# A two-layer hybrid trunk on eight cores: block-diagonal recurrence gates as two full matmuls instead of four in quadrants, with a newly drawn instruction order

## The chip, the cores and the metric

The kernel runs on all 8 cores of one Trainium2 chip. Each core takes one prompt (16 learned meta tokens and 2048 prompt tokens) and 16 short sample sequences of 8 tokens: 2192 columns in all. Every core holds the same weights' program and reads them for itself. The metric is the device time in microseconds of the slowest core, the median of several executions.

## The reference, cut to what matters

Two layers, each with a feed-forward, a mixer and a second feed-forward; the change lies in the mixer's gated recurrence:

```python
for l in range(DEPTH):
    x = x + 0.5 * swiglu(rmsnorm(x, norm_ffn1[l]), w_ffn1_gu[l], w_ffn1_down[l])
    m, cb, hl, S = mixer(rmsnorm(x, norm_mix[l]), ...)
    x = x + m
    x = x + 0.5 * swiglu(rmsnorm(x, norm_ffn2[l]), w_ffn2_gu[l], w_ffn2_down[l])

def rg_lru(x, h0, pos, wa, ba, wx, bx, lam):
    xb = x.reshape(B, L, LRU_BLOCKS, LRU_BW)          # 8 blocks of 64 channels
    r = sigmoid(einsum('blnc,ncd->blnd', xb, wa).reshape(B, L, D_LRU) + ba)
    i = sigmoid(einsum('blnc,ncd->blnd', xb, wx).reshape(B, L, D_LRU) + bx)
    a = exp(-LRU_C * r * softplus(-lam))
    bt = sqrt(1 - a * a) * (i * x)                    # reset at position 0
    h_t = a_t * h_(t-1) + bt_t                        # scan over positions
```

The width is 1024, the feed-forward's 2816, the recurrence's 512: four slices of 128 channels, each of them two of the 64-wide blocks. The mixer's other half is a gated linear attention with four heads (queries and keys of 64, values of 128), in chunks.

## The kernel before, in words

Everything is kept transposed: channels on the 128 partitions, tokens along the free dimension. The residual stream `x` stays in SBUF for the whole program. The 2192 columns are cut into six tiles, `TILES`, of 256, 384, 384, 384, 400 and 384 columns, and these into two halves of three. The feed-forwards of the first half work in two tiles of 512 columns (`"w0"`, `"w1"`), the very first one from its third group of weights on; its first two groups run over tiles 0, 1 and 2 (`UNITS0`). Those of the second half work in the three tiles. In the first layer the mixer of one half is interleaved with the feed-forward of the other, and so on through the program, so that TensorE finds dense matmuls while ScalarE and VectorE work on a mixer.

Weights come from HBM, converted to bf16, over GpSimd's DMA queue into rings of slots: `rgu` (gate and up, 6 slots), `rdn` (down, 5 slots), `rpg` (the mixer's pages, 6 slots; its load is `load_page`, line 547). A slot's load is issued when the last matmul that reads the slot is done. PSUM has eight banks `ps`, given out by class (`VT`): the mixer's products are of class "M", at most four at a time.

`lru(c)` is the recurrence of one slice of 128 channels of a tile. It runs 4 slices x 6 tiles x 2 layers = 48 times. It projects, convolves on VectorE (`xc`), makes a bf16 copy `xb`, and multiplies that by the block-diagonal gate weights `bd` for `r` (first half of `bd`) and `i` (second half). Before, each of the two products is two matmuls of 64x64, one for each block, and the four of them lie in the four quadrants of the array. Block `hf` of gate `wh` lands in partitions `(hf ^ wh) * 64`, so that gate `i` comes out with its two halves of partitions exchanged. Two activations over 64 partitions each (line 991) exchange them back, while `r` is one activation of 128 partitions; its bias column is permuted to match.

No order is written by hand. `Sched` takes the list of operations, with a duration for each, and simulates the five engines: at each step it gives each engine the ready operation with the best key. The key has a priority, the length of the path behind the operation, and a perturbation: the program is cut into windows of 25,000 ns of the simulated time, and `PLAN` has a number for each, from which `policy` draws offsets for sixteen kinds of operations (`kind`), the weight of a switch of ScalarE's table, a random amount and how many banks stay for the down-projection. So the numbers in `PLAN` and the durations decide the order on every engine, the place of each DMA among GpSimd's additions, and the PSUM bank of each product. Within an engine's stream instructions run strictly in that order, with semaphore waits between engines.

Line 489 is the matmul helper, 470 the activation helper, 476 and 482 VectorE's two helpers, 592 GpSimd's addition of squares for a norm, 533 and 540 the loads of feed-forward weights, 882 the load of `bd`, once a layer.

Of the kernel before, what the change touches and what calls it, by code (L numbers as in the profile page):

```python
# [32 lines left out]
UNITS0 = [(0, 0), (0, 1), (1, 0), (1, 1), (0, 2), (1, 2)]  # L33
FIRST = ["x0", "x1", "g0", "g1", "d0", "d1", "g2", "x2", "g3", "d2", "g4", "d3", "d4", "g5", "d5", "g6", "d6", "g7", "d7", "g8", "d8"]
EARLY = 4
PLAN = [788770747, 0, 992418779, 673166238, 0, 781246477, 774010218, 0, 522389631, 334221663, 985327654, 932172178, 62324483, 0,
# [7 lines left out]
EPS = 1e-6  # L44
NCOLS = 136
NPAGE = 28
# [337 lines left out]
def build_program(cfg):  # L384
# [4 lines left out]
    wmx_d = nc.dram_tensor("wmx", [2, NPAGE, 128, 1024], F32, kind="ExternalInput").ap()  # L389
    wlr_d = nc.dram_tensor("wlr", [2, 128, 256], F32, kind="ExternalInput").ap()  # L390
    cols_d = nc.dram_tensor("cols", [128, NCOLS], F32, kind="ExternalInput").ap()
    bd_d = nc.dram_tensor("bdw", [2, 128, 512], F32, kind="ExternalInput").ap()
    wg2_d = nc.dram_tensor("wg2", [2, 128, 256], F32, kind="ExternalInput").ap()
    st0_d = nc.dram_tensor("st0", [2, 128, 256], F32, kind="ExternalInput").ap()
    S0_d = nc.dram_tensor("S0", [2, 2, 4, 128, 512], F32, kind="ExternalInput").ap()
# [8 lines left out]
    with es:  # L404
# [10 lines left out]
        cols = sb("cols_sb", [128, NCOLS], F32)  # L415
        ones = sb("ones", [128, 128], BF16)
        cst = sb("cst", [128, 928], BF16)
        bd = sb("bd", [128, 8, 64], BF16)
        wg2b = sb("wg2b", [128, 256], BF16)
        wlr = sb("wlr_sb", [128, 256], BF16)  # L420
        sm = sb("sm", [128, 64], F32)
# [42 lines left out]
        def bk(v):  # L464
            return psum[v.bank]
# [414 lines left out]
        def layer_setup(l):  # L880
            P.op("sp", lambda h: h.dma_start(out=st0[:], in_=st0_d[l]), [("go", 3, 0)], writes=["st0"], dur=60, sem=named_sem("st0"), nbytes=131072, prio=1)
            P.op("pool", lambda h: h.dma_start(out=bd[:].rearrange("p a b -> p (a b)"), in_=bd_d[l]), reads=[("go", 4, 0)], writes=["bd"], dur=600,
                 sem=named_sem("bd"), nbytes=128 * 2048, prio=1.5)
            P.op("pool", lambda h: h.dma_start(out=wlr[:], in_=wlr_d[l]), reads=[("go", 4, 0)], writes=["wlr"], dur=600, sem=named_sem("wlr"), nbytes=65536, prio=1.5)
            P.op("pool", lambda h: h.dma_start(out=wg2b[:], in_=wg2_d[l]), reads=[("go", 4, 0)], writes=["wg2b"], dur=600, sem=named_sem("wg2b"), nbytes=16384, prio=1.5)

# [5 lines left out]
        def mixer_tile(l, ti):  # L892
# [57 lines left out]
            def lru(c):  # L950
# [27 lines left out]
                else:  # L978
# [3 lines left out]
                act(xb.ap[:, :n], xc.ap[:, :n], AF.Copy, n, [xc.r], [xb.r])  # L982
                yield
                ra, it = Fa(), Fa()
                v2 = [VT("M"), VT("M")]
                P.op("pe", [mm(v2[wh], bd[hf * 64:hf * 64 + 64, wh * 4 + c, :], xb.ap[hf * 64:hf * 64 + 64, :n], n,
                               out=lambda wh=wh, r0=(hf ^ wh) * 64: bk(v2[wh])[r0:r0 + 64, :n]) for wh in range(2) for hf in range(2)],
                     [xb.r, "bd"], v2, dur=95 + 1.2 * mmd(n), prio=0)
                act(ra.ap[:, :n], lambda: bk(v2[0])[:, :n], AF.Tanh, n, [v2[0], "sm2"], [ra.r], scale=0.5, bias=sm2[:, l * 4 + c:l * 4 + c + 1], tbl="S")
                bo = 8 + l * 4 + c  # L990
                P.op("act", [lambda h, r0=r0: h.activation(out=it.ap[64 - r0:128 - r0, :n], in_=bk(v2[1])[r0:r0 + 64, :n], func=AF.Tanh, scale=0.5,  # L991
                                                           bias=sm2[r0:r0 + 64, bo:bo + 1]) for r0 in (0, 64)],
                     [v2[1], "sm2"], [it.r], dur=2 * ac(n), tbl="S", prio=1, deps=(None, None))
                xb.done()
                am = Fa()
                c1 = sm[:, l * 4 + c:l * 4 + c + 1]
# [375 lines left out]
def build_weights(inp):  # L1372
    wgu = np.empty((4, NJ, 128, 2048), np.float32)
    wdn = np.empty((4, NJ, 128, 1024), np.float32)
    wmx = np.empty((2, NPAGE, 128, 1024), np.float32)
    wlr = np.zeros((2, 128, 8, 32), np.float32)
    bdw = np.zeros((2, 128, 8, 64), np.float32)
    for l in range(2):
        for f, (gu, dn) in enumerate([(inp["w_ffn1_gu"][l], inp["w_ffn1_down"][l]), (inp["w_ffn2_gu"][l], inp["w_ffn2_down"][l])]):
            for j in range(NJ):  # L1380
                wgu[l * 2 + f, j, :, 0:1024] = _chunk_cols(gu, j * 128).reshape(128, 1024)
                wgu[l * 2 + f, j, :, 1024:2048] = _chunk_cols(gu, DFF + j * 128).reshape(128, 1024)
                wdn[l * 2 + f, j] = dn[j * 128:(j + 1) * 128, :]
        win = inp["w_in"][l]
        for k in range(12):
            wmx[l, k] = _chunk_cols(win, k * 128).reshape(128, 1024)
        for i in range(4):
            wmx[l, 12 + i] = win[i * 256:(i + 1) * 256, 1536:2048].reshape(2, 128, 512).transpose(1, 0, 2).reshape(128, 1024)
        for h4 in range(4):
            wmx[l, 16 + h4] = _chunk_cols(win, 2048 + h4 * 128).reshape(128, 1024)  # L1390
        for mc in range(8):
            wmx[l, 20 + mc] = _chunk_cols(inp["w_out"][l], mc * 128).reshape(128, 1024)
        wlr[l, :, :, :16] = _chunk_cols(win, 2560, 16)
        for wh, wname in enumerate(("lru_wa", "lru_wx")):
            for c in range(4):
                for hf in range(2):
                    bdw[l, hf * 64:(hf + 1) * 64, wh * 4 + c] = inp[wname][l, 2 * c + hf]
    return {"wgu": wgu, "wdn": wdn, "wmx": wmx, "wlr": wlr.reshape(2, 128, 256), "bdw": bdw.reshape(2, 128, 512)}

def build_cols(inp):  # L1400
    c = np.zeros((128, NCOLS), np.float32)

    def put(col, vec, nch):
        c[:, col:col + nch] = vec.reshape(nch, 128).T

    for l in range(2):
        b = l * 64
        put(b + 0, inp["norm_ffn1"][l], 8)
        put(b + 8, inp["norm_mix"][l], 8)
        put(b + 16, inp["norm_ffn2"][l], 8)  # L1410
        for k in range(4):
            put(b + 24 + k * 4, inp["lru_conv_w"][l][k], 4)
        put(b + 40, inp["lru_conv_b"][l], 4)
        put(b + 44, inp["lru_ba"][l], 4)
        put(b + 48, inp["lru_bx"][l].reshape(4, 2, 64)[:, ::-1].reshape(-1), 4)
        put(b + 52, inp["lru_lambda"][l], 4)
        put(b + 56, inp["gla_b_gate"][l], 2)
        put(b + 58, inp["gla_norm"][l], 1)
    put(128, inp["norm_final"], 8)
    return c  # L1420
# [63 lines left out]
```

How the kernel before makes its waits and increments, by code:

```python
            def body(h, name=name):  # L1347
                for k, (waits, fn, inc) in enumerate(out[name]):
                    if name == "sp" and k == past:
                        for sem, val in fin[0]:
                            h.wait_ge(sem, val)
                    for sem, val in waits[:-1] if name in ("act", "dve") else waits:
                        h.wait_ge(sem, val)
                    i = fn(h)
                    if name in ("act", "dve") and waits:
                        i = i.wait_op(waits[-1][0], waits[-1][1], "sem-ge")
                    if inc is not None:
                        i.then_inc(inc[0], inc[1])
                if name == "sp":
                    for sem, val in fin[1]:
                        h.wait_ge(sem, val)
                if name == "pool":
                    for sem in gu_sem + dn_sem + pg_sem:
                        h.wait_ge(sem, P.dcnt[id(sem)])
```

## Time and profile before

| | before |
|---|---|
| median of 3 runs | 2510.01 us (2509.41 to 2564.43) |
| profiled execution, its own time | 2509.41 us |
| its span, slowest core (core 5) | 2507.3 us |
| TensorE matmul busy | 2479.1 us, 99% |
| VectorE busy | 1533.7 us, 61% |
| ScalarE busy | 1320.1 us, 53% |
| GpSimd busy | 628.8 us, 25% |
| share of TensorE in the chain that ended last | 92% |

The profiled execution took 2.1 us more than the span of its slowest core, which is what lies around the program's own instructions. The busy time of TensorE counts a matmul from its start to its modelled end; in a dense stream each overlaps the next, so what a matmul costs is read from the distance between two starts, not from its own duration.

### The profile page before, as it was taken

To read this page: it belongs to the slowest core of one execution; us is meant where nothing else is said; L and a number is where in the kernel's file an instruction comes from. 1 tells how busy PE (TensorE), PEld (TensorE's weight loads), DVE (VectorE), ACT (ScalarE), POOL (GpSimd) and SP (SyncE) were. 2 spreads that over 40 slices of the span, in tenths; PEclk is the share of its full clock that TensorE was granted. 3 is DMA by queue.
4 is the path that set the end of the run, shared out by engine and by line. 5 is a ranking of instruction groups with operands and counts; after the bars stand their busy time and mean duration, and the time that the engine had idled before them with its cause. 6 is when DMAs were issued, how large, how long until landed. Compare 5 with 4: busy or idle time off the path is not lost.

```text
span 2507.3 us, 42427 instructions; the slowest of 8 cores (2499.4 to 2507.3 us)
## 1 busy us (share of the span) xinstructions
PE 2479.1 (99%) x14673; PEld 1349.2 (54%) x14673; DVE 1533.7 (61%) x3016; ACT 1320.1 (53%) x2507; POOL 628.8 (25%) x1011
## 2 busy tenths in 40 slices
PE   7999999999999999999999999999999999999998
PEld 4444565555544444444555556655554444555556
DVE  6444765657766679444753367666576666886346
ACT  2312678676868675311311148685678686753114
POOL 2212331213322313301200042422151413142002
PEclk9999999999999999999999999999999999999999
DMA  9666577666867897465344447767566787786322
GB/s 186 125 109 93 93 119 108 99 103 96 121 102 110 124 150 129 74 94 85 60 72 68 65 75 106 120 100 118 94 99 104 109 126 112 143 134 138 51 43 78
DMA packets 118173, 259.28 MB, mean 103 GB/s; under 512 B 12912, under 2 KB 23664, under 8 KB 117968
## 3 DMA queue, kind: packets, MB, share of 16 engines
q0 software_dynamic: 104576, 238.38, 61.2%
q1 hardware_dynamic: 12672, 17.59, 2.1%
q8 instruction: 127, 2.08, 0.3%
q14 instruction: 78, 0.64, 0.1%
q10 hardware_dynamic: 720, 0.59, 0.1%
HBM read 472.21 MB, written 13.65 MB: 194 GB/s over the span
## 4 chain that ended last, share of the span: by engine, by line
PE 92%; ACT 4%; DVE 1%; issue 1%; DMA 1%; POOL 0%; DVEq 0%; POOLq 0%; ACTq 0%
PE ps L489 91%; PE ps L488 1%; ACT Fb L470 1%; DMA rgu<-wgu 1%; DVE x L476 1%; ACT L470 1%; ACT Fb L991 1%; ACT L999 0%; ACT sg L470 0%; ACT Bb L470 0%; ACT Fb L999 0%; PE ps L1194 0%; DVE Fb L476 0%; ACT Fb L1000 0%; POOL x L498 0%
## 5 line engine op out<-in xcount | busy, mean ns | idle before, releaser
L489 PE MATMUL ps<-xn,rgu 128*128 128x384 bf16 (+4 forms) x6896 | 1312.9, 346 | 1.2 <-DMA rgu<-wgu 0.9
L489 PEld LDWEIGHTS ps<-xn,rgu 128*128 128x128 bf16 x6896 | 669.9, 98 | 574.4 <-issue 7.7
L476 DVE SCALAR_TENSOR_TENSOR x<-ps,x 128x384 f32<-128x384 f32 (+5 forms) x1056 | 609.0, 601 | 239.2 <-PE ps L489 220.3
L489 PE MATMUL ps<-hb,rdn 128*128 128x384 bf16 (+4 forms) x3384 | 677.5, 346 | 0.7 <-ACT Fb L470 0.3
L470 ACT ACTIVATE sg<-ps 128x384 f32<-128x384 f32 (+5 forms) x451 | 234.2, 525 | 787.2 <-PE ps L489 672.9
L482 DVE TENSOR_TENSOR hb<-ps,sg 128x384 bf16<-128x384 f32 (+5 forms) x451 | 266.8, 600 | 386.4 <-PE ps L489 330.9
L489 PEld LDWEIGHTS ps<-hb,rdn 128*128 128x128 bf16 x3384 | 327.0, 98 | 276.5 <-issue 8.6
L547 POOL DMA_DIRECT2D rpg<-wmx x336 | 180.1, 539 | 683.2 <-PE ps L489 621.4
L489 PE MATMUL ps<-xnt,rpg 128*128 128x384 bf16 (+3 forms) x1536 | 262.1, 318 | 0.4 <-ACT Fb L470 0.3
L533 POOL DMA_DIRECT2D rgu<-wgu x168 | 90.7, 540 | 615.3 <-PE ps L489 602.0
L470 ACT ACT_TABLE_LOAD x149 | 191.2, 1283 | 26.0 <-PE ps L489 21.6
L489 PEld LDWEIGHTS ps<-xnt,rpg 128*128 128x128 bf16 x1536 | 147.5, 98 | 94.5 <-issue 3.4
L470 ACT ACTIVATE sqf<-x 128x384 bf16<-128x384 f32 (+3 forms) x244 | 106.7, 471 | 142.6 <-DVE x L482 69.7
L540 POOL DMA_DIRECT2D rdn<-wdn x166 | 88.8, 546 | 324.9 <-PE ps L489 319.9
L476 DVE SCALAR_TENSOR_TENSOR Fb<-Fb,cols_sb 128x384 f32<-128x384 f32 (+3 forms) x216 | 122.8, 577 | 72.6 <-ACT Fb L470 39.3
L470 ACT ACTIVATE Fb<-ps 128x384 f32<-128x384 f32 (+5 forms) x262 | 112.9, 463 | 37.9 <-PE ps L489 28.5
L489 PE MATMUL ps<-mixin,rpg 128*128 128x384 bf16 (+3 forms) x768 | 126.0, 319 | 0.0
L476 DVE SCALAR_TENSOR_TENSOR Fb<-Fb 128x384 f32<-128x384 f32 (+2 forms) x144 | 84.3, 587 | 68.0 <-ACT Fb L991 42.5
L476 DVE SCALAR_TENSOR_TENSOR xn<-x,cols_sb,ps 128x256 bf16<-128x256 f32 (+3 forms) x216 | 105.7, 547 | 8.4 <-ACT ps L625 8.4
L489 PEld LDWEIGHTS ps<-mixin,rpg 128*128 128x128 bf16 x768 | 75.3, 98 | 46.3 <-issue 1.3
L592 POOL TENSOR_TENSOR rsf<-rsf,sqf 128x384 f32<-128x384 f32 (+3 forms) x116 | 91.8, 807 | 32.1 <-ACT sqf L470 31.3
L592 POOL TENSOR_TENSOR rsf<-sqf 128x384 f32<-128x384 bf16 (+3 forms) x58 | 47.6, 821 | 127.6 <-ACT sqf L470 120.0
(141 smaller groups left out, 1757.8 us busy)
## 6 DMA issues: line engine op xcount, KB each, us to landing
rgu<-wgu POOLq DMA_DIRECT2D x168, 512.0 KB, 7.3
rpg<-wmx POOLq DMA_DIRECT2D x336, 256.0 KB, 6.5
rdn<-wdn POOLq DMA_DIRECT2D x166, 256.0 KB, 7.2
x<-xT POOLq DMA_DIRECT2D x8, 768.0 KB, 9.8
yT<-Fb SPq DMA_DIRECT2D x24, 192.0 KB, 5.0
rpg<-wgu POOLq DMA_DIRECT2D x7, 512.0 KB, 9.5
S0f<-S SPq DMA_DIRECT2D x12, 256.0 KB, 8.9
Sos<-S0f SPq DMA_DIRECT2D x12, 256.0 KB, 5.1
```

The lines of the kernel that those rows point to most:

```text
L470: P.op("act", lambda h: h.activation(out=o_(), in_=i_(), func=func, scale=scale, **kw), reads, writes, dur=ac(n, ptr, 0 if callable(in_) e ...
L476: P.op("dve", lambda h: h.scalar_tensor_tensor(out=o_(), in0=a_(), scalar=scalar, in1=b_(), op0=op0, op1=op1), reads, writes, dur=dv(n, 0 ...
L482: P.op("dve", lambda h: h.tensor_tensor(out=o_(), in0=a_(), in1=b_(), op=op), reads, writes, dur=dv(n), prio=prio, port=not (callable(in0) ...
L488: return lambda h: h.matmul(o_(), lhsT=lhsT, rhs=rhs, start=start, stop=stop, skip_group_check=True)
L489: return lambda h: h.matmul(o_(), lhsT=lhsT, rhs=rhs, start=start, stop=stop)
L533: P.op("pool", lambda h: h.dma_start(out=s.ap.rearrange("p (a b) -> p a b", a=2), in_=wgu_d[fi, j].rearrange("p (a b) -> p a b", a=2)), wr ...
L540: P.op("pool", lambda h: h.dma_start(out=s.ap, in_=wdn_d[fi, j]), writes=s.keys, dur=600, sem=s.sem, nbytes=128 * 1024 * 4, prio=prio)
L547: P.op("pool", lambda h: h.dma_start(out=rpg[:, s, :], in_=wmx_d[l, k]), reads=[("go", 5, min(pg_n[0] // 3, 2))], writes=[("pg", s)], dur= ...
L592: P.op("pool", lambda h: h.tensor_tensor(out=out, in0=a, in1=b, op=ALU.add), reads, writes, dur=pl(self.n), prio=0, port=True)
L991: P.op("act", [lambda h, r0=r0: h.activation(out=it.ap[64 - r0:128 - r0, :n], in_=bk(v2[1])[r0:r0 + 64, :n], func=AF.Tanh, scale=0.5, bias ...
```

## The change

The gate product of `lru` becomes one full 128x128 matmul for each of the two gates. The weight page `bd` holds each pair of blocks as a 128x128 matrix with zeros beside the diagonal, so it has 8 x 128 columns instead of 8 x 64, and its DMA reads 512 KB instead of 256 KB of float32 from HBM. Each gate has its own bank, taken when its matmul is given out, and one activation over 128 partitions. The bias of gate `i` is not permuted any more. The duration that `Sched` is told is twice one matmul's instead of `95 + 1.2 * mmd(n)` for the four. `PLAN` has other numbers throughout, of which a line is shown. The tiling of the feed-forwards, the rings and all other operations are as before.

```diff
-PLAN = [788770747, 0, 992418779, 673166238, 0, 781246477, 774010218, 0, 522389631, 334221663, 985327654, 932172178, 62324483, 0,
+PLAN = [301746851, 0, 1013753834, 374752431, 0, 211164062, 689418677, 0, 0, 919143051, 683213839, 630184684, 126345493, 892550642,
...
-        bd = sb("bd", [128, 8, 64], BF16)
+        bd = sb("bd", [128, 8, 128], BF16)
...
-                 sem=named_sem("bd"), nbytes=128 * 2048, prio=1.5)
+                 sem=named_sem("bd"), nbytes=128 * 4096, prio=1.5)
...
-                v2 = [VT("M"), VT("M")]
-                P.op("pe", [mm(v2[wh], bd[hf * 64:hf * 64 + 64, wh * 4 + c, :], xb.ap[hf * 64:hf * 64 + 64, :n], n,
-                               out=lambda wh=wh, r0=(hf ^ wh) * 64: bk(v2[wh])[r0:r0 + 64, :n]) for wh in range(2) for hf in range(2)],
-                     [xb.r, "bd"], v2, dur=95 + 1.2 * mmd(n), prio=0)
-                act(ra.ap[:, :n], lambda: bk(v2[0])[:, :n], AF.Tanh, n, [v2[0], "sm2"], [ra.r], scale=0.5, bias=sm2[:, l * 4 + c:l * 4 + c + 1], tbl="S")
-                bo = 8 + l * 4 + c
-                P.op("act", [lambda h, r0=r0: h.activation(out=it.ap[64 - r0:128 - r0, :n], in_=bk(v2[1])[r0:r0 + 64, :n], func=AF.Tanh, scale=0.5,
-                                                           bias=sm2[r0:r0 + 64, bo:bo + 1]) for r0 in (0, 64)],
-                     [v2[1], "sm2"], [it.r], dur=2 * ac(n), tbl="S", prio=1, deps=(None, None))
+                for wh, dst in ((0, ra), (1, it)):
+                    v = VT("M")
+                    P.op("pe", mm(v, bd[:, wh * 4 + c, :], xb.ap[:, :n], n), [xb.r, "bd"], [v], dur=mmd(n), prio=0)
+                    bo = wh * 8 + l * 4 + c
+                    act(dst.ap[:, :n], lambda v=v: bk(v)[:, :n], AF.Tanh, n, [v, "sm2"], [dst.r], scale=0.5, bias=sm2[:, bo:bo + 1], tbl="S")
...
-                    bdw[l, hf * 64:(hf + 1) * 64, wh * 4 + c] = inp[wname][l, 2 * c + hf]
+                    bdw[l, hf * 64:(hf + 1) * 64, wh * 4 + c, hf * 64:(hf + 1) * 64] = inp[wname][l, 2 * c + hf]
...
-        put(b + 48, inp["lru_bx"][l].reshape(4, 2, 64)[:, ::-1].reshape(-1), 4)
+        put(b + 48, inp["lru_bx"][l], 4)
```

What the order looks like on TensorE where the recurrence of the second mixer tile's first two slices runs among a feed-forward of the other half (`xn,rgu` is its gate or up product, `xnt,rpg` and `rpg,xnt` projections of the mixer, `vtm,kendT` the attention's state update, which writes 64 partitions for each head). Before:

```order
L489 MATMUL ps<-rpg,xnt 128x512 x8
L489 MATMUL ps<-Bb,bd 64x384 x4
L489 MATMUL ps<-rpg,xnt 128x512 x16
...
L489 MATMUL ps<-xn,rgu 128x400 x8
L489 MATMUL ps<-xn,rgu 128x384 x16
L489 MATMUL ps<-Bb,bd 64x384 x4
L489 MATMUL ps<-vtm,kendT 64x128 x6
```

And in the changed kernel, at the same two gate products:

```order
L489 MATMUL ps<-rpg,xnt 128x512 x8
L489 MATMUL ps<-Bb,bd 128x384 x2
L489 MATMUL ps<-rpg,xnt 128x512 x16
...
L1190 MATMUL ps<-cst,Bb 128x128 x3
L489 MATMUL ps<-xn,rgu 128x400 x8
L489 MATMUL ps<-Bb,bd 128x384 x2
L489 MATMUL ps<-vtm,kendT 64x128 x6
```

Each gate product is two rows' worth of full matmuls at nearly the same place; what stands before the second one has changed. In the whole stream 7 of the 48 gate products stand directly before `vtm,kendT` before, and 8 of 48 now.

On VectorE at the very start of the program (squares of tile 1, `sqf<-x 128x384`, among the normalized columns of tile 0, `xn 128x256`, and of tile 1), before:

```order
L482 TENSOR_TENSOR sqf<-x 128x384
L476 SCALAR_TENSOR_TENSOR xn<-x,cols_sb,ps 128x256 x3
L482 TENSOR_TENSOR sqf<-x 128x384
L476 SCALAR_TENSOR_TENSOR xn<-x,cols_sb,ps 128x256 x2
L482 TENSOR_TENSOR sqf<-x 128x384
L476 SCALAR_TENSOR_TENSOR xn<-x,cols_sb,ps 128x384 x8
L482 TENSOR_TENSOR hb<-ps,sg 128x256 x2
```

Now:

```order
L476 SCALAR_TENSOR_TENSOR xn<-x,cols_sb,ps 128x256 x3
L482 TENSOR_TENSOR sqf<-x 128x384 x2
L476 SCALAR_TENSOR_TENSOR xn<-x,cols_sb,ps 128x256 x5
L482 TENSOR_TENSOR sqf<-x 128x384
L476 SCALAR_TENSOR_TENSOR xn<-x,cols_sb,ps 128x384 x4
L482 TENSOR_TENSOR hb<-ps,sg 128x256
L476 SCALAR_TENSOR_TENSOR xn<-x,cols_sb,ps 128x384 x4
```

The last square of tile 1 now stands behind five normalizations of tile 0 in a row, and on TensorE the matmul that takes it stands behind the first six of the first feed-forward product.

On GpSimd where `bd` is loaded for the first time and the mixer's pages begin, before:

```order
L882 DMA bd<-bdw 128x512
L885 DMA wg2b<-wg 128x256
L884 DMA wlr_sb<-wlr 128x256
L540 DMA rdn<-wdn 128x1024 x3
L498 DMA x<-xT 128x4x384 x2
L533 DMA rgu<-wgu 128x2048 x3
L547 DMA rpg<-wmx 128x1024 x2
L540 DMA rdn<-wdn 128x1024 x2
L547 DMA rpg<-wmx 128x1024 x4
```

Now:

```order
L885 DMA wg2b<-wg 128x256
L884 DMA wlr_sb<-wlr 128x256
L882 DMA bd<-bdw 128x1024
L540 DMA rdn<-wdn 128x1024 x3
L498 DMA x<-xT 128x4x384 x2
L533 DMA rgu<-wgu 128x2048 x3
L547 DMA rpg<-wmx 128x1024 x2
L540 DMA rdn<-wdn 128x1024 x2
L547 DMA rpg<-wmx 128x1024 x3
L533 DMA rgu<-wgu 128x2048
L547 DMA rpg<-wmx 128x1024
```

The larger load of `bd` goes behind two small ones, and one load of a feed-forward slot has moved ahead of the sixth page. Shifts of this size run through the whole stream: of about 500 rows on GpSimd and 1500 on TensorE most stand a few places away from where they stood.

## Rows read from the trace of the kernel before

**Rows 1.** The cores' spans and mean granted TensorE clock.

```profile
core 1: 2500.4 us, clock 0.999
core 5: 2507.3 us, clock 0.995
die 0 (median of its cores): 2500.2 us, clock 0.999
die 1 (median of its cores): 2506.9 us, clock 0.995
```

**Rows 2.** Windows of core 5, all engines (PE, PEld, DVE, ACT, POOL busy, clock, DMA).

```profile
60.00:2480.00 2420.00, 2415.43 (x14166) 1305.38 (x14165) 1480.89 (x2882) 1289.03 (x2439) 606.82 (x973) 1.00 0.63 101
```

**Rows 3.** What PE waited for from 60 to 2480 us (total, times, longest).

```profile
PE ps L489 <- ACT Fb L470: 0.7, 2, 0.3
PE ps L489 <- DVE hb L482: 0.6, 2, 0.4
PE ps L489 <- DVE Bb L476: 0.6, 1, 0.6
PE ps L489 <- POOL Bb L592: 0.6, 2, 0.3
PE ps L488 <- DVE Fb L476: 0.5, 2, 0.3
PE ps L489 <- DVE Bb L482: 0.5, 1, 0.5
```

**Rows 4.** PE in order of time, core 5: start, duration, count, idle before.

```profile
19.05 2.83 PE L489 MATMUL ps<-xn,rgu 128*128 128x256 bf16 x16
22.73 0.49 PE L489 MATMUL ps<-xn,rgu 128*128 128x256 bf16 x3 [0.85 <-DMA rgu<-wgu]
...
54.11 1.46 PE L489 MATMUL ps<-xn,rgu 128*128 128x384 bf16 x8
55.41 1.14 PE L489 MATMUL ps<-hb,rdn 128*128 128x384 bf16 x6
...
2471.17 5.40 PE L489 MATMUL ps<-xn,rpg 128*128 128x256 bf16 x48
2476.41 0.33 PE L489 MATMUL ps<-sqf,ones 128*128 128x400 bf16 x1
```

**Rows 5.** PE around a gate product of 384 columns.

```profile
430.80 0.98 PE L489 MATMUL ps<-xn,rgu 128*128 128x384 bf16 x5
431.70 0.36 PE L489 MATMUL ps<-Bb,bd 64*64 64x384 bf16 x4
431.99 0.85 PE L489 MATMUL ps<-hb,rdn 128*128 128x400 bf16 x4
432.68 0.33 PE L489 MATMUL ps<-xnt,rpg 128*128 128x384 bf16 x1
```

**Rows 6.** PE around a gate product of 256 columns.

```profile
277.61 0.81 PE L489 MATMUL ps<-xn,rgu 128*128 128x384 bf16 x4
278.35 0.30 PE L489 MATMUL ps<-Bb,bd 64*64 64x256 bf16 x4
278.58 0.82 PE L489 MATMUL ps<-rpg,xnt 128*128 128x512 bf16 x3
```

**Rows 7.** PE where a gate product stands beside a state update.

```profile
408.71 1.14 PE L489 MATMUL ps<-xn,rgu 128*128 128x384 bf16 x6
409.78 0.36 PE L489 MATMUL ps<-Bb,bd 64*64 64x384 bf16 x4
410.06 0.36 PE L489 MATMUL ps<-vtm,kendT 128*64 128x128 bf16 x6
410.36 1.15 PE L489 MATMUL ps<-xn,rgu 128*128 128x384 bf16 x6
```

**Rows 8.** ACT's groups for the gates of 384 columns (busy, mean ns, idle before).

```profile
L991 ACT ACTIVATE Fb<-ps,sm 64x384 f32<-64x384 f32 x64 | 36.9, 576 | 2.7 <-PE ps L489 1.1
L470 ACT ACTIVATE Fb<-ps,sm 128x384 f32<-128x384 f32 x32 | 18.5, 578 | 12.4 <-PE ps L489 12.3
```

**Rows 9.** DMA issues: KB each, median us to landing; and GpSimd's additions.

```profile
rpg<-wmx POOLq DMA_DIRECT2D x336, 256.0 KB, 6.5
L592 POOL TENSOR_TENSOR rsf<-rsf,sqf 128x384 f32<-128x384 f32 (+3 forms) x116 | 91.8, 807 | 32.1 <-ACT sqf L470 31.3
```

**Rows 10.** POOL's page loads in order of time, and PE's use of them.

```profile
622.26 0.54 POOL L547 DMA_DIRECT2D rpg<-wmx  x1 [5.71 <-PE ps L489]
...
627.99 1.46 PE L489 MATMUL ps<-xnt,rpg 128*128 128x384 bf16 x8
```

**Rows 11.** Windows of core 5, PE alone: busy, granted clock, DMA share, GB/s.

```profile
33.00:48.00 15.00, 14.74 (x82) 0.81 1.06 170
249.00:264.00 15.00, 15.00 (x70) 0.81 0.29 50
350.00:365.00 15.00, 15.00 (x88) 0.81 0.92 144
```

More of the change, by code:

```diff
@@ L391, in build_program @@
     cols_d = nc.dram_tensor("cols", [128, NCOLS], F32, kind="ExternalInput").ap()
-    bd_d = nc.dram_tensor("bdw", [2, 128, 512], F32, kind="ExternalInput").ap()
+    bd_d = nc.dram_tensor("bdw", [2, 128, 1024], F32, kind="ExternalInput").ap()
     wg2_d = nc.dram_tensor("wg2", [2, 128, 256], F32, kind="ExternalInput").ap()
@@ L1376, in build_weights @@
     wlr = np.zeros((2, 128, 8, 32), np.float32)
-    bdw = np.zeros((2, 128, 8, 64), np.float32)
+    bdw = np.zeros((2, 128, 8, 128), np.float32)
     for l in range(2):
@@ L1396, in build_weights @@
                 for hf in range(2):
-                    bdw[l, hf * 64:(hf + 1) * 64, wh * 4 + c] = inp[wname][l, 2 * c + hf]
-    return {"wgu": wgu, "wdn": wdn, "wmx": wmx, "wlr": wlr.reshape(2, 128, 256), "bdw": bdw.reshape(2, 128, 512)}
+                    bdw[l, hf * 64:(hf + 1) * 64, wh * 4 + c, hf * 64:(hf + 1) * 64] = inp[wname][l, 2 * c + hf]
+    return {"wgu": wgu, "wdn": wdn, "wmx": wmx, "wlr": wlr.reshape(2, 128, 256), "bdw": bdw.reshape(2, 128, 1024)}
 def build_cols(inp):
```

14 rows, old and new, of the table PLAN are left out of this document.

## The prediction

> **What bounds the kernel now.** I read the cores first, then the busy shares by stage, then what TensorE waits for, and last the distances between its matmuls. The cores say which one to look at: core 5 of the second die, 2507.3 us, while the first die needs 2500.2 us [rows 1]. That gap is no work of the program. Three stretches of 15 us on core 5 were granted a TensorE clock of 0.81, between the chip's two levels of 1.2 and 2.4 GHz, in the middle of dense matmuls [rows 11]; a matmul stream slowed to 0.81 loses 0.19 of each stretch, 3 x 15 x 0.19 = 8.5 us, about the 6.7 us by which the dies differ.
>
> The stage view leaves one engine. From 60 to 2480 us TensorE is busy for 2415.4 of 2420 us, VectorE for 1481, ScalarE for 1289, GpSimd for 607 [rows 2]. TensorE's idle time there is the 3.5 us of the waits view, six kinds with a longest of 0.6 us [rows 3]. So the time is the sum of TensorE's distances from start to start, plus some 23 us before the steady stream and 8 us after it. An engine beside TensorE can return at most the few microseconds of rows 3, and a microsecond of TensorE's stream is a microsecond of the kernel. A gain of 50 us (2%, about what a measurement of this kernel can tell from no change) isn't there to be had by an edit of 48 small products.
>
> The price of a plain matmul comes from two neighbours in time: eight of 384 columns from 54.11 to 55.41 us, 0.163 us each; forty-eight of 256 from 2471.17 to 2476.41, 0.109 us each [rows 4]. For 400 columns I take 400/384 of the first, 0.170.
>
> **The gate products on TensorE.** This is the term that carries the sum. Four 64x64 matmuls show a busy time of 0.36 us together, barely over one matmul's own 0.347, so they run side by side. What they cost is seen in their neighbours [rows 5]. From 430.80 five plain matmuls ought to last 5 x 0.163 = 0.81 us, and the quadrants begin after 0.90: 0.09 us lost ahead. The next plain matmul starts 0.29 us after them. The four of 400 behind need 0.69 instead of 0.68: 0.01. In all 0.39 us. Two full matmuls of 384 cost 2 x 0.163 = 0.326. The edit therefore returns 0.064 us for a product of 384 columns, though it doubles the columns streamed through the array: the quadrants save 0.163 us of streaming and pay about 0.23 us for entering and leaving their mode. At 256 columns [rows 6]: 0.74 - 0.65 = 0.09 ahead, 0.23 inside, 0.01 behind, 0.33 in all against 0.218, a return of 0.11. At 400 it is 0.40 against 0.340, a return of 0.06.
>
> Seven products stand directly before the attention's state update, which writes 64 partitions and has to leave the full mode anyway. There the entry is shared [rows 7]: 1.07 - 6 x 0.163 = 0.09 ahead, 0.28 for the quadrants, 0.30 for the update; the update alone would keep 0.09 + 0.30, so the product costs 0.28 there, and two full matmuls cost 0.045 us more. In the new order eight products stand there, at no extra price, since the update pays for its own entry.
>
> The sum: 48 products are 32 of 384 columns, 8 of 400 and 8 of 256; 25 x 0.064 + 8 x 0.06 + 8 x 0.11 - 7 x 0.045 = 1.60 + 0.48 + 0.88 - 0.32 = 2.6 us less on TensorE. All of it is on the path.
>
> The Trainium skill speaks against this edit: "TensorEngine Tiling (Array Packing)", section Theoretical Speedup, gives 2x for each dimension of at most 64 and hence four quadrants in the time of one. Its section Key Properties says that a change of tiling mode drains the engine, without a price. By the first alone each product would now cost a whole matmul more; the trace agrees that the four run side by side and puts a price of about 0.23 us on the drain, which is the larger of the two.
>
> **ScalarE.** Gate `i` was two activations of 64 partitions, 0.576 us each, as long as the one of 128 for `r`, 0.578 [rows 8]. One instead of two returns about 0.57 x 48 = 27 us of busy time (somewhat less at 256). It lies beside TensorE's work: 1289 of 2420 us are busy. What it can give is a shorter recurrence chain, at most the waits in rows 3 that come from the mixer's chain. I book 0 and keep the whole of rows 3 for the range.
>
> **DMA and banks.** `bd` is 256 KB more, once a layer; a page of 256 KB lands in 6.5 us [rows 9], and the first gate product comes at 278 us, over 100 us after the load's place in GpSimd's stream. Nobody waits for it; its price without that cover would be some 6 us, once. The two gates take their banks one after the other instead of both at once, which can only ease the limit of four.
>
> **The start.** VectorE now makes the last square of tile 1 after five normalizations. Each of these takes 0.43 us, so the square comes some 0.8 us later, and the matmul that takes it splits the first feed-forward product. Before, TensorE was done with the first sixteen at 21.9 and stood 0.85 us, to 22.73, for the second slot of weights [rows 4]. The loads' order up to there is unchanged, so 22.73 stands and the delay falls into that wait. Price without the cover: 0.8 us. The normalized columns of tile 1 come 1.2 us later too, near 25.5; the product that needs the last of them gets there at 22.73 + 16 x 0.109 + 7 x 0.163 = 25.6. I book 0, and up to 1 us in the range.
>
> **The new order.** It touches everything, and no row prices it beforehand. What it can change is TensorE's idle time and the small losses around it. Below: all of rows 3 gone, 3.5 us, and as much again because a matmul that starts after a wait isn't overlapped by the one before (0.163 us a time, over 20 places), so -7 us. Above: twice as much waiting, +7 us, is my bound for an order that hides as well as the old one. I take 0: both orders have the same dependencies and the same engines at 25 to 61% beside TensorE.
>
> Sum: 2509.41 - 2.6 = 2506.8 us against the profiled execution. The median of the runs is 0.6 higher, and I forecast **2507 us**.
>
> **The rivals.**
>
> *Page loads slip (slower).* The mixer's weights arrive with nothing to spare. The page issued at 622.26 lands by the median of 6.5 us at about 628.8, or a little earlier, and the product that starts at 627.99 is of its kind [rows 9, 10]; six slots and a rule of "issue when the last reader is done" make this the normal case. If the new order puts one more of GpSimd's additions (0.807 us) ahead of a page that is used on landing, TensorE stands for that long. Once in each of the 12 mixer tiles this is 12 x 0.81 = 9.7 us: 2516.5 us; twice, 2526. It decides from the point at which issue to first use drops under the landing time. Against it: the page loads wait for TensorE nearly always, not for an addition, and rows 3 show no wait for a page at all. Chance 0.15.
>
> *The mixer's chain stops showing.* ScalarE's 27 us and single banks remove the waits that come from mixer products. All of rows 3 and the restart losses gone: 2506.8 - 7 = 2500 us. For it: five of the six rows of waits name a mixer buffer or a norm. Against: other waits would take their place. Chance 0.12.
>
> *The packing rule holds.* The 0.09 us ahead and the tail behind a quadrant group belong to neighbours that would be there anyway, and a full product costs a whole matmul more: +0.163 x 32 + 0.17 x 8 + 0.109 x 8 = 7.5 us, 2517 us. Against it: the same loss ahead in rows 5, 6 and 7 with three different followers. The section Theoretical Speedup of "TensorEngine Tiling (Array Packing)" in the Trainium skill would have it so. Chance 0.05.
>
> *No gain, since the mode changes stay.* If the two full matmuls were separated by tiled work, or the drain moved to whoever is next, the time would be 2509.5 us. In the order nearly all pairs stand together, 40 of 48 between full matmuls. Chance 0.08.
>
> **How the numbers follow.** The forecast (2503 to 2511) has 0.58, the rivals 0.15, 0.12, 0.05 and 0.08, and 0.02 is for something large. The clock adds a width of its own: without the three stretches of 0.81 the slowest core would be at the first die's 2500; with twice as many it would be 8 us above. The range of 2499 to 2516 takes in the low rival, the packing rule nearly, the lower part of the first rival and most of the clock's width, and leaves out about 2 in 10. All cases but the last lie within 2%: same 0.97, slower 0.02, faster 0.01.
>
> **What the next profile would show.** The gate product as two of 128x384 with 0.326 us from its start to the next matmul's and no loss ahead: if there is a loss, the first step is wrong. TensorE's busy time 3 to 4 us lower, 14,577 matmuls; ScalarE's about 27 us lower. TensorE's waits between 60 and 2480 us near 3.5 us: over 10 us, above all for pages, would be the first rival. The first sixteen matmuls of the feed-forward ending in a wait for weights to 22.7 us. Stretches at 0.81: as many as before, or the comparison of the slowest cores is off by 2.8 us for each. Wrong altogether would be a stage in which TensorE stands for several microseconds.

## The result and the profile after

The changed kernel took 2497.3 us (median), the kernel before 2509.9 us beside it: 0.995 of it, 95% interval 0.9928 to 0.9973, so 12.6 us less. In two later comparisons on other chips it was 0.9960 (0.9944 to 0.9976) and 0.9962 (0.9950 to 0.9975), 10.1 and 9.6 us less. Every time and difference from here on is a median over the executions in which no die ran long at a lower clock, while the expectations quoted below reckon with medians over all executions, which lie up to 1 us beside them. The direction was forecast, the size was not: 2.6 us were expected, and 2497.3 lies under the range's lower end of 2499.

The changed kernel's page: the share of each engine, the chain that ended last, and the cores' spans, which answer to [rows 1].

```profile
span 2496.5 us, 42211 instructions; the slowest of 8 cores (2490.1 to 2496.5 us)
PE 2473.0 (99%) x14577; PEld 1357.6 (54%) x14577; DVE 1522.7 (61%) x3016; ACT 1287.1 (52%) x2459; POOL 628.5 (25%) x1011
PE 98%; DVE 1%; DMA 0%; ACT 0%; POOL 0%; issue 0%; DVEq 0%; ACTq 0%; POOLq 0%
die 0 (median of its cores): 2490.9 us, clock 0.999
die 1 (median of its cores): 2494.7 us, clock 0.997
```

TensorE's share of the chain went from 92 to 98%; ScalarE's, 4% before, is gone. ScalarE's busy time is 33 us lower, where 27 were forecast. The undisturbed die went from 2500.2 to 2490.9 us.

TensorE's stage from 60 to 2480 us (window), what it waited for there (waits), and a gate product in order of time; these answer to [rows 2], [rows 3] and [rows 5].

```profile
60.00:2480.00 2420.00, 2418.82 (x14182) 1322.05 (x14181) 1475.08 (x2896) 1260.86 (x2402) 608.33 (x974) 1.00 0.62 102
```

```profile
PE ps L489 <- DVE xn L476: 1.0, 5, 0.2
```

```profile
418.92 1.46 PE L489 MATMUL ps<-xn,rgu 128*128 128x384 bf16 x8
420.21 0.49 PE L489 MATMUL ps<-Bb,bd 128*128 128x384 bf16 x2
420.54 1.46 PE L489 MATMUL ps<-xnt,rpg 128*128 128x384 bf16 x8
```

Eight matmuls take 1.29 us to the gate's start, 0.161 each: nothing is lost ahead. The two full ones take 0.33. The ten waits of the kernel before are gone; eight of them ended on a mixer buffer or a norm, two on a feed-forward's hidden values `hb`. The five that are left, 0.2 us each, are of another place, the normalized columns of a feed-forward's first product at 2244 us.

**Where the time went.** Rows of idle time understate a wait: the matmul after it is not overlapped by the one before. And a matmul can start late with so little idle time, or none, that the waits view doesn't list it at all; the shortest that it lists is 0.2 us. In the kernel before, ahead of a projection of the mixer:

```profile
282.44 1.63 PE L489 MATMUL ps<-hb,rdn 128*128 128x384 bf16 x9
284.10 1.03 PE L489 MATMUL ps<-xnt,rpg 128*128 128x256 bf16 x8
```

Nine of 384 columns need 9 x 0.163 = 1.47 us and the next starts after 1.66: 0.19 us are lost, and no idle time stands beside the second row. So I added, over all matmuls, the distance from each start to the next less the distance that its shape has in a dense stream (0.163 us at 384 columns, 0.216 at 512, 0.169 at 400, 0.109 at 256), and sorted the rest by what stands there. For core 5, 2507.3 us before and 2496.3 after:

| part of core 5's difference | us |
|---|---|
| the 48 gate products, with what they cost their neighbours | -2.4 |
| TensorE kept waiting between 22 us and the end, restarts included | -4.6 |
| stretches of lower clock | -2.3 |
| from the last matmul to the last store | -1.4 |
| the first 22 us | -0.3 |
| sum | -11.0 |

How the sum is divided between clock, waits and products is good to about half a microsecond, since a matmul in a slow stretch can have waited as well. Core 1 ran at full clock on both sides and is the cleaner of the two: of its 10.0 us, 2.3 are the products with their neighbours, 5.5 the waits, 2.0 the way from the last matmul to the last store and 0.2 the first 22 us. Of the waits the larger part was never in [rows 3]: from 60 to 2470 us on core 5 the late starts that the waits view doesn't list came to 5.4 us before and 1.7 after.

The clock term is in the windows of the changed kernel, which answer to [rows 11]. The stretch at 33 us is missing and the two others are there. The rows are of core 4, the slowest; there, behind the waits at 2244 us, 3.4 us more ran at 0.50, the lower of the two levels. Core 5 of the table had no such stretch.

```profile
248.00:263.00 15.00, 15.00 (x70) 0.81 0.33 57
348.00:363.00 15.00, 15.00 (x96) 0.82 0.74 124
2247.00:2250.40 3.40, 3.40 (x13) 0.50 0.24 78
```

That leaves two causes to tell apart. The waits can have gone because the edit takes work from ScalarE, or because the new numbers drew a better order.

### The profile page after: what moved, and what is told of

Same layout as the page of the kernel before. It is cut to its first block, busy times and chain, and to the rows that moved or that the text cites. A ratio compares the mean times of both kernels' runs of the same rounds, so it can differ in the third digit from the quotient of the medians.

```text
span 2496.5 us, 42211 instructions; the slowest of 8 cores (2490.1 to 2496.5 us)
## 1 busy us (share of the span) xinstructions
PE 2473.0 (99%) x14577; PEld 1357.6 (54%) x14577; DVE 1522.7 (61%) x3016; ACT 1287.1 (52%) x2459; POOL 628.5 (25%) x1011
## 4 chain that ended last, share of the span: by engine, by line
PE 98%; DVE 1%; DMA 0%; ACT 0%; POOL 0%; issue 0%; DVEq 0%; ACTq 0%; POOLq 0%
PE ps L489 97%; PE ps L488 1%; DMA rgu<-wgu 0%; DVE xn L476 0%; PE ps L1190 0%; DVE x L476 0%; POOL x L498 0%; DVE S0f L476 0%; DVE sqf L482 0%; ACT L624 0%; ACT Bb L470 0%; ACT ps L624 0%; ACT Fb L470 0%; ACT ps L625 0%; DVE hb L482 0%
```

## The experiments

The old order can be kept exactly. It follows from the durations told to the scheduler and from `PLAN`, not from the instructions, so one operation of two full matmuls with the old duration leaves every engine's stream as it was. All the runs named "old order" have that stream, instruction by instruction, and those named "new order" the changed kernel's. Each was measured against the kernel before on the same chip.

**Run 1: the edit in the old order.** The kernel before, with

```diff
-                P.op("pe", [mm(v2[wh], bd[hf * 64:hf * 64 + 64, wh * 4 + c, :], xb.ap[hf * 64:hf * 64 + 64, :n], n,
-                               out=lambda wh=wh, r0=(hf ^ wh) * 64: bk(v2[wh])[r0:r0 + 64, :n]) for wh in range(2) for hf in range(2)],
+                P.op("pe", [mm(v2[wh], bd[:, wh * 4 + c, :], xb.ap[:, :n], n) for wh in range(2)],
...
-                P.op("act", [lambda h, r0=r0: h.activation(out=it.ap[64 - r0:128 - r0, :n], ...) for r0 in (0, 64)],
-                     [v2[1], "sm2"], [it.r], dur=2 * ac(n), ...)
+                P.op("act", [lambda h: h.activation(out=it.ap[:, :n], ...)],
+                     [v2[1], "sm2"], [it.r], dur=2 * ac(n), ...)
```

> The gate products are two full 128x128 matmuls and one activation for each gate, as in the changed kernel, but the order of every engine is that of the kernel before, instruction by instruction, since the durations told to the scheduler and PLAN are the old ones. Theory 1 (the edit returns what its 48 products cost less on TensorE, and the drawn order returned the rest): 2.4 to 2.8 us less than the kernel before on each die, near 2507, TensorE's idle time after the start still about 3.5 us, ScalarE's busy time some 27 us lower. Theory 2 (the 27 us of ScalarE's time shorten the mixer's chain, and that removed the waits): 6 to 8 us less than before, near 2503, with TensorE's idle time after the start close to the 1.3 us of the changed kernel.

Measured: 2496.1 against 2504.7 us, 0.9964 (0.9950 to 0.9978), so 8.6 us less. Theory 1 is out; theory 2 had the right side and named too little. A chip later, beside the changed kernel itself:

> The edit in the old order once more, beside the changed kernel on one chip. It gave 9.0 us in its first run, the changed kernel 9.6 us on another chip. If the drawn order adds nothing, both lie within 1 us of each other here; if it adds what the first comparison suggested, the changed kernel is 2 us or more ahead.

Measured: 2494.2 against 2503.8 us, 0.9963 (0.9950 to 0.9976), 9.6 us less. And the changed kernel on that chip and on the one before it:

> The changed kernel, unaltered, beside the run before this one: 9 to 10 us less than the kernel before, 0.996 of it, and 0 to 1 us less than the edit in the old order. Its gain on the first chip was 12.3 us, of which 2 to 3 us would be stretches of lower clock if this theory is right, so no more than 10.5 here unless the kernel before shows three such stretches again.

> The changed kernel once more, unaltered, beside the next two kernels and the kernel before on one chip, to see what the drawn order adds to the edit. The edit alone, in the old order, gave 9.0 us against the kernel before on the chip of the runs before this one. Theory 1 (the drawn order returned most): 12 us less than before, with 3 us or more from the order. Theory 3 (the edit gives nearly all in either order, and the rest of the first comparison lay in stretches of lower clock and in the last store): 9 to 11 us less than before.

Measured: 2494.2 against 2503.8, 0.9962 (0.9950 to 0.9975), and 2493.3 against 2503.4, 0.9960 (0.9944 to 0.9976). On the one chip that ran both, the drawn order adds nothing to the edit: 9.6 us with it and 9.6 without. The 12.6 us of the first comparison had some 2 to 3 us of clock in them, as the table shows for core 5; the two later profiles of the changed kernel have a mean clock of 0.999 on every core.

**Run 2: ScalarE's part put back.** As run 1, but gate `i` by two activations of 64 partitions, without the exchange.

```diff
+                P.op("act", [lambda h, r0=r0: h.activation(out=it.ap[r0:r0 + 64, :n], in_=bk(v2[1])[r0:r0 + 64, :n], ...) for r0 in (0, 64)],
```

> As the run before it, but gate i is still made by two activations of 64 partitions each, without the exchange, so that ScalarE has as much to do as in the kernel before; only TensorE's products change. Theory 1: the same time as the run before it within 0.5 us, some 2507. Theory 2: 2507 as well, but 4 to 5 us slower than the run before it. TensorE's busy time in both as in the changed kernel; 0.326 us for a product of 384 columns and nothing lost ahead of it.

Measured: 2500.4 us, 0.9982 (0.9972 to 0.9992): 4.3 us less than the kernel before, 4.3 more than run 1. That is the step of 4 to 5 us that theory 2 named; the level, 2507, is too high in both theories. The waits view of the slowest core hardly tells the two runs apart, 2.2 us in 6 waits against 2.3 in 7; the late starts that it doesn't list went from 1.7 to 4.8 us on core 5.

**Run 3: ScalarE's part alone.** The kernel before, quadrants and all, with one activation for gate `i`; the exchange of the two halves of partitions is left out.

> The kernel before, in its own order and with its four quadrant products, but gate i is made by one activation over 128 partitions. It leaves out the exchange of the two halves of partitions, so gate i goes to the wrong half of the channels; the work of every other instruction is as before. It takes ScalarE's 27 us alone out of the kernel before. Theory 3 (a shorter ScalarE leg in the recurrence removes half of TensorE's waits): 4 to 5.5 us less than before. Theory 1 (ScalarE is covered): 0 to 1 us less.

Measured: 2496.6 against 2503.4 us, 0.9973 (0.9962 to 0.9984), 6.9 us less, more than either theory named. Without any change to TensorE's products, most of the gain is there.

**Run 4: work given back to ScalarE, at another place.** Run 3 with an idle copy of 64 partitions added where the scan is over.

```diff
+                    P.op("act", [lambda h: h.activation(out=scr[:, :n], in_=hs.ap[0:64, :n], func=AF.Copy, scale=1.0),
+                                 lambda h: h.activation(out=hprev[:, c:c + 1], in_=hs.ap[:, n - 1:n], func=AF.Copy, scale=1.0)],
```

> The run with the old order, the quadrants and one activation for gate i (whose exchange of the two halves is left out), which took 6.8 us off the kernel before, with 48 idle copies of 64 partitions added on ScalarE just before the copy of the scan's last column. ScalarE is as busy as in the kernel before, but the work stands behind the recurrence's chain instead of in its middle. If ScalarE's occupancy as such makes TensorE wait, all of the 6.8 us come back and it equals the kernel before. If only the length of the leg from the gate product to the scan counts, it stays 5 to 7 us below. In between if other chains of the mixer run behind that place on ScalarE.

Measured: 2498.2 against 2503.8 us, 0.9979 (0.9969 to 0.9988), 5.6 us less. ScalarE is busy for 1303 us instead of 1286, which is only half of the way back to the 1320 of the kernel before, so the expectation's "as busy as" was not met. If occupancy as such were the price, about 3.4 of the 6.9 us would have come back; 1.2 did, across two chips. So most of the gain is not ScalarE's occupancy, but where in the recurrence the work stands. In the traces of core 1 the time from a gate product's first matmul to the end of the last exponential, mean of 48, is 7.07 us before, 6.23 in run 3, 6.26 here, 6.30 in run 1 and 5.96 in the changed kernel. One activation less is 0.8 us off that leg.

**Run 5: one activation more.** Run 2 with gate `r` in two halves as well.

> The full products in the old order, with two activations of 64 partitions for gate i and two for gate r, none of them exchanging halves: ScalarE has 27 us more to do than in the kernel before and 54 more than with one activation a gate. If each 27 us of ScalarE's work in the chain costs alike, 4 to 6 us more than with three activations (which was 4.1 us below before), so equal to the kernel before or up to 2 us above. If the waits have a floor and the first 27 us were just at an edge, 1 us or less more.

Measured: 2520.9 against 2503.4 us, 1.0071 (1.0057 to 1.0084), 17.5 us more. The leg is 7.77 us. What TensorE waited for from 60 to 2480 us:

```profile
PE ps L489 <- DVE Bb L476: 2.4, 3, 1.2
PE ps L488 <- DVE Fb L476: 2.3, 3, 0.9
PE ps L489 <- DVE hb L482: 2.2, 5, 0.7
PE ps L489 <- DVE mixin L476: 2.2, 5, 0.6
PE ps L488 <- ACT Sb L470: 1.3, 2, 0.7
```

Three of these five kinds stand in [rows 3] too; in all there are 39 waits of 20.7 us against 10 of 3.5. With two, three and four activations the edit in the old order stands at -8.6, -4.3 and +17.5 us. The price of one more half activation for each product (29 and 34 us of ScalarE's busy time) went from 4.3 to 21.8 us, and the listed waits from 7 to 39: in an order cut close, a further delay of the same length finds many more places without slack.

One place shows it. It is where the attention's first product of the tile of 400 columns waits for `Bb`, TensorE's rows in order of time, here in the kernel before:

```profile
766.19 1.03 PE L489 MATMUL ps<-hb,rdn 128*128 128x512 bf16 x4
767.85 0.45 PE L489 MATMUL ps<-Bb 64*16 64x16 bf16 x8 [0.63 <-DVE Bb L476]
```

Four of 512 columns take 4 x 0.216 = 0.86 us, so 0.80 us are lost ahead of the second row. In run 1:

```profile
758.35 1.03 PE L489 MATMUL ps<-hb,rdn 128*128 128x512 bf16 x4
759.30 0.45 PE L489 MATMUL ps<-Bb 64*16 64x16 bf16 x8
```

0.09 us are lost, and no wait: as much as ahead of the quadrants in [rows 5], the entry into the smaller mode. In run 2:

```profile
759.70 1.03 PE L489 MATMUL ps<-hb,rdn 128*128 128x512 bf16 x4
761.17 0.45 PE L489 MATMUL ps<-Bb 64*16 64x16 bf16 x8 [0.44 <-DVE Bb L476]
```

0.61 us. And in run 5:

```profile
763.65 1.03 PE L489 MATMUL ps<-hb,rdn 128*128 128x512 bf16 x4
765.90 0.45 PE L489 MATMUL ps<-Bb 64*16 64x16 bf16 x8 [1.23 <-DVE Bb L476]
```

1.39 us. So this place alone follows the leg step by step. This product isn't of the recurrence at all. How the leg's length reaches it is in the chain that ended last, of the kernel before, its longer pieces in order of time from 746 us:

```profile
746.57 0.60 ACT Fb L991
749.22 1.28 ACT L999
750.52 0.72 ACT Fb L999
751.24 0.61 ACT Fb L1000
...
758.95 1.28 ACT L1113
760.24 0.60 ACT Fb L1113
...
763.76 1.28 ACT L1130
766.14 0.97 DVE Bb L476 x3
767.87 2.56 PE ps L489 x20
```

It begins with a half activation of gate `i` (L991), goes on through the recurrence's exponentials (L999, L1000) and only then comes to the attention's (L1113, L1130), whose result VectorE needs for `Bb`: ScalarE works them off in its queue's order.

**Runs 6 and 7: the new order.** The changed kernel with the quadrants and two activations back, and with full products and two activations.

```diff
-                    P.op("pe", mm(v, bd[:, wh * 4 + c, :], xb.ap[:, :n], n), [xb.r, "bd"], [v], dur=mmd(n), prio=0)
+                    P.op("pe", [mm(v, bd[hf * 64:hf * 64 + 64, wh * 4 + c, hf * 64:hf * 64 + 64], xb.ap[hf * 64:hf * 64 + 64, :n], n,
+                                   out=lambda v=v, r0=(hf ^ wh) * 64: bk(v)[r0:r0 + 64, :n]) for hf in range(2)],
+                         [xb.r, "bd"], [v], dur=mmd(n), prio=0)
```

> The new order, instruction by instruction, with the gate products in the four quadrants of 64x64 again and two activations of 64 partitions for gate i, so that what is left of the change is the drawn order alone. Theory 1: 2.4 to 2.8 us slower than the changed kernel, near 2500, and still about 9 us faster than the kernel before; TensorE's idle time after the start near 1.5 us. Theory 2: TensorE's waits come back with ScalarE's longer work, 2504 to 2506. If a pair of products does not run side by side in the new order, because it is given out as two operations, it costs up to 0.16 us more for each such product.

> The changed kernel's order and full products, with two activations of 64 partitions for gate i. The quadrants with two activations in this order were 4.4 us slower than the kernel before, and the changed kernel 9.6 us faster, so products and activations together are worth 14 us in this order. If the activations carry most of it, as 4.9 of 9.0 us in the old order, this one lies 7 to 9 us above the changed kernel; if the products do, 3 us above it.

Measured: 2509.4 against 2504.7 us, 1.0017 (1.0008 to 1.0026), 4.7 us more than the kernel before and above what either theory named; and 2500.1 against 2503.8, 0.9985 (0.9976 to 0.9994), 3.7 us less, between the two cases. So the new order with the old work is worse than the old order, and the edit is worth 14 us in it: 5.9 for the activation and, across two chips, 8.4 for the products. Of the 8.4 about 2.4 are TensorE's own; the rest is waiting time, 5.6 us more than before in run 6 on core 1 by the sum of distances, and 0.6 less in run 7. In the old order too the products gave more than their own 1.9 us when ScalarE had three activations (4.3 us), and 1.8 to 2.7 when it had two. Why full products spare TensorE waits beyond their own time was not settled: the leg is as long with them (7.02 us in run 2, 7.07 before).

**Runs 8 and 9: other draws.** The changed kernel with the `PLAN` of the kernel before, and with `PLAN = [0]`.

> The changed kernel with the PLAN numbers of the kernel before: another drawn order for the same work. If any order hides the work beside TensorE as well as any other, within 2 us of the changed kernel, 2496 to 2500. If the new PLAN is a particularly good draw, the waits of TensorE after the start come to 5 to 20 us and the time to 2503 to 2520.

> The changed kernel with a PLAN of zeros, so that no window's order is perturbed: the order that the durations and priorities alone give. With the numbers of the kernel before the changed kernel took 60 us more than with its own, TensorE standing for several microseconds at a time around 1870 and 2240 to 2310 us. If that is what an order costs that isn't picked for its durations, this one lies 30 to 90 us above the changed kernel, with TensorE idle in the same places; if the old numbers were an unlucky draw, within 15 us.

Measured: 2565.7 us, 1.0243 (1.0223 to 1.0262), 61 us more than the kernel before, hence some 70 more than the changed kernel and far above both cases; and 2548.7 us in one execution against 2503.4, 45 us more than the kernel before and 55 more than the changed kernel. TensorE's longest kinds of waits, from 60 to 2480 us, with the old numbers:

```profile
PE ps L489 <- DVE mixin L476: 13.0, 3, 6.5
PE ps L489 <- DVE xn L476: 8.8, 5, 4.2
```

and with zeros:

```profile
PE ps L482 <- DVE xn L469: 14.2, 6, 4.6
PE ps L482 <- DVE x L469: 10.6, 17, 1.6
```

A single wait of 6.5 us, and 49.6 and 29.6 us of idle time in all. The rest is largely clock. Where TensorE stood for so long, the granted clock fell to 0.50, as around the wait of 5.8 us that ends at 1878.31 us with the old numbers:

```profile
1868.00:1875.00 7.00, 3.23 (x15) 1.00 0.27 49
1875.00:1881.00 6.00, 2.69 (x9) 0.54 0.00 0
```

On the slowest core 54.6 us ran at 0.50 with the old numbers and 44.2 with zeros, which costs up to half of that. Two draws that weren't chosen for these durations cost 55 and 70 us against the new one. The new numbers keep what there was, since the edit's new durations would shuffle the order; they add nothing to it. That they were picked by a search is what these two runs suggest, not something that they show.

## Why the prediction was wrong, point by point

**What bounds the kernel, and that 50 us aren't there to be had: right.** Every difference found lies in TensorE's stream, its waits, the clock or the last store.

**The gate products, 2.6 us: right, a little high.** The sum over the 48 products and their neighbours gives 2.4 us on core 5, by the distances of both profiles; 1.9 in run 1, where seven of them still share their place with the state update. Reading their price from the neighbours' starts, instead of from the rows' own 0.36 us, gave both sign and size, and the rival that the packing rule holds is out: no plain matmul was lost ahead of a gate, 0.33 us inside it.

**ScalarE, "I book 0": the step that failed.** It is worth 6.9 us by itself in the old order (run 3), 4.3 beside full products (runs 1 and 2) and 5.9 in the new order. The reason given, that 1289 of 2420 us are busy and so it lies beside TensorE's work, is an average over the span. The change acts on the leg from the gate product to the scan, which delays everything behind it in ScalarE's queue, and that delay reached TensorE in the ten waits of [rows 3] and in more late starts that [rows 3] doesn't list. Hence "at most the waits in rows 3" was no bound either: they are 3.5 us, with ten restarts of 0.163 us 5.1 us. The forecast counted 20 restarts where ten waits stand, and its 7 us came near the truth by that slip. The rival "the mixer's chain stops showing" was this mechanism, at a chance of 0.12. Its 7 us stand against 4.6 on core 5, 5.5 on core 1 and about 6.5 in run 1. It should have been the forecast: with the products' 2.6 us it gives 2500, 9.6 us less than before, and the later chips show 9.6 and 10.1.

**The new order, 0 us: the value right, its bounds wrong.** It adds nothing to the edit, but as a sum of terms that the forecast did not have. In the profiles with the old order the program ends 7.67 us after the last matmul on every core, in those with the new order 5.4 to 7.0 us, so the new order gains 1 to 2 us there; it gives most of that back at the start (below). And the bound of +7 us for "an order that hides as well as the old one" rested on engines that are 25 to 61% busy; two other draws cost 55 and 70 us more than the chosen one. The rows of the kernel before could not have priced that, and the range and the chance of a slower kernel were too confident for an order that was not known to be chosen.

**The start, "I book 0, and up to 1 us in the range": not absorbed.** TensorE's rows at the start of the changed kernel, which answer to [rows 4]:

```profile
17.32 1.44 PE L489 MATMUL ps<-xn,rgu 128*128 128x256 bf16 x6 [1.05 <-DMA rgu<-wgu]
18.55 0.53 PE L489 MATMUL ps<-sqf,ones 128*128 128x384 bf16 x1
18.87 4.51 PE L489 MATMUL ps<-xn,rgu 128*128 128x256 bf16 x27
24.37 5.23 PE L489 MATMUL ps<-xn,rgu 128*128 128x384 bf16 x31 [0.99 <-DVE xn L476]
```

The wait for weights now stands ahead of the first product and not behind the first sixteen, and the late square costs nothing: on core 5 the first 22 us are 0.3 us shorter. But the last row waits 0.99 us for the normalized columns of tile 1. This wait stands on nearly every core of the profiles with the new order, 0.2 to 1.5 us long, and with the old order on a single one, 0.2 us. The forecast had these columns 0.1 us ahead of their product.

**The clock: a term that I put into the range alone.** It gave 2 to 3 us of the first comparison on core 5. The low end of the range took in the waits or the clock, not both: 2506.8 less 7 us of waits less 2.8 us for one stretch (0.19 x 15.1) would be 2497.0, close to the 2497.3 measured, partly by luck since the 7 us were counted too high. The page loads of the rival "page loads slip" never showed: no wait for a page stands in the waits of the changed kernel.

## What to carry to other kernels

When one engine is 99% busy and the rest of its time is a dozen short waits, the chain behind those waits can already be uncovered: here shortening it paid until the waits were gone, and lengthening it by the same amount cost several times more. Share of busy time says nothing about that. Count the waits, add for each the overlap that the next instruction loses, look also for starts that come late without a listed wait, and ask which chain they end on. An edit can be told from the order in which a scheduler puts it by keeping the durations that the scheduler is told. And an order that is good for one set of durations need not be good for another: with the edit's durations, the old numbers cost 61 us against the kernel before.

## What the hardware showed that was not expected

- An activation over 64 partitions takes as long as one over 128: 0.576 against 0.578 us at 384 columns [rows 8], and 0.8 us of the chain for each.
- Four 64x64 matmuls side by side in the four quadrants cost 0.39 us at 384 columns, of which 0.09 ahead of them and 0.29 to the next start, against 0.33 for two full ones. Doing twice the columns was cheaper than entering and leaving the mode.
- A granted clock of 0.81 came in short stretches, mostly on one die while the other ran at full clock with the same matmuls: of 15.1 us in the first comparison, three on each core of the second die before and one or two after; of 3.7 to 7.8 us on another chip, three to five on each core of the first die (runs 1, 2, 6 and 8; in run 8 the second die had one of 15.2 us as well); and none in the profiles of the two last chips. Two of the long stretches cost core 5 2.6 us each by the distances between its matmuls; the one at 33 us cost about 1.8, since TensorE was kept waiting there on the other die too.
- A wait of several microseconds costs more than itself: with the old numbers 49.6 us of listed idle time went with 54.6 us at a granted clock of 0.50, with zeros 29.6 with 44.2.
